# Two transformer blocks: the root of the query/key norm as logarithm and exponential, and a new order of steps around it

## The reference, cut to what matters

```python
def rms_norm(x, g):
    xf = x.astype(jnp.float32)
    y = xf * lax.rsqrt(jnp.mean(xf * xf, axis=-1, keepdims=True) + RMS_EPS)
    return (y * g.astype(jnp.float32)).astype(x.dtype)

def fox_attention(u, w_in, b_f, q_norm_g, k_norm_g, w_out):      # 16 heads of 64, 1024 tokens
    q, k, v, g, fl = jnp.split(u @ w_in, ...)
    q = rms_norm(q, q_norm_g) * (FOX_HD ** -0.5)
    k = rms_norm(k, k_norm_g)
    f_cum = jnp.cumsum(jax.nn.log_sigmoid(fl + b_f), axis=1)
    s = q @ k.T + f_cum[t] - f_cum[s]                            # causal
    o = softmax(s) @ v
    return (o * jax.nn.sigmoid(g)) @ w_out

# in each layer, after the mixer:
x = layer_norm(ALPHA * x + gate * y, ln_g[layer, 0], ln_b[layer, 0])
y = jnp.square(jax.nn.relu(u @ mlp_w1[layer] + mlp_b1[layer])) @ mlp_w2[layer] + mlp_b2[layer]
```

## Time and profile before

| | |
|---|---|
| median of 3 runs | 3938.67 us (3938.32 to 3942.71) |
| the profiled execution, its own time | 3946.69 us |
| its span in the profile | 3945.0 us |
| PE busy | 3705.5 us (94%), 18038 matmuls |
| DVE, ACT, POOL busy | 2020.8 us (51%), 1143.6 us (29%), 2117.1 us (54%) |
| TensorE clock granted, mean | 0.97 |

### The profile page before, as it was taken

How to read it: one execution, slowest core, us unless ns; L and a number is a source line. 1 busy time by engine, 2 the same in 40 slices (tenths; PEclk the granted TensorE clock), 3 DMA queues, 4 the chain that set the end, 5 groups by cost and what they waited for, 6 DMA issues and landing times. The chain is left out here.

```text
span 3945.0 us, 49917 instructions
## 1 busy us (share of the span) xinstructions
PE 3705.5 (94%) x18038; PEld 2988.6 (76%) x18038; DVE 2020.8 (51%) x3309; ACT 1143.6 (29%) x1852; POOL 2117.1 (54%) x1786
## 2 busy tenths in 40 slices
PE   6898989999999889999988999999998889999997
PEld 5677877888888667777766878888787768888886
DVE  6864463333344567777765122222499564444445
ACT  5432231111112544455433111111315132222222
POOL 3643368666663333333326866665495495646462
PEclk8999989999999999999998999999999999999999
DMA  6320112333220011111111211111021111212121
GB/s 223 98 86 27 33 43 70 99 101 97 90 85 23 23 38 38 44 43 39 43 38 32 59 48 48 48 48 48 27 59 43 43 39 52 64 32 64 33 62 43
DMA packets 248500, 224.57 MB, mean 57 GB/s; under 512 B 12660, under 2 KB 194578, under 8 KB 248355
## 3 DMA queue, kind: packets, MB, share of 16 engines
q1 hardware_dynamic: 222240, 171.09, 14.4%
q10 hardware_dynamic: 26115, 51.53, 4.2%
HBM read 218.33 MB, written 4.26 MB: 56 GB/s over the span
## 5 line engine op out<-in xcount | busy, mean ns | idle before, releaser
L3164 POOL TENSOR_SCALAR WH<-RAW 128x1024 fp32r<-128x1024 f32 x255 | 721.1, 2828 | 1034.0 <-issue 342.8
L713 PE MATMUL PS<-UH,WH 128*128 128x512 f32 (+1 forms) x2192 | 866.4, 395 | 21.9 <-POOL WL L3167 14.2
L715 PE MATMUL PS<-UH,WL 128*128 128x512 f32 (+1 forms) x2192 | 860.2, 392 | 0.0
L714 PE MATMUL PS<-UL,WH 128*128 128x512 f32 (+1 forms) x2192 | 859.9, 392 | 0.0
L3167 POOL TENSOR_TENSOR WL<-RAW,WH 128x256 fp32r<-128x256 f32 x1017 | 790.1, 808 | 21.3
L2183 DVE TENSOR_TENSOR X<-PS,X 128x512 f32<-128x512 f32 x432 | 292.5, 687 | 436.2 <-PE PS L845 424.3
L713 PEld LDWEIGHTS PS<-UH,WH 128*128 128x128 f32 (+1 forms) x2192 | 414.7, 189 | 114.6 <-issue 13.9
L715 PEld LDWEIGHTS PS<-UH,WL 128*128 128x128 f32 (+1 forms) x2192 | 414.0, 189 | 89.4
L714 PEld LDWEIGHTS PS<-UL,WH 128*128 128x128 f32 (+1 forms) x2192 | 414.7, 189 | 86.7 <-issue 0.2
L843 PE MATMUL PS<-WH,HH 128*128 128x512 f32 x1024 | 404.4, 395 | 16.8 <-DVE X L2183 13.4
L844 PE MATMUL PS<-WH,HL 128*128 128x512 f32 x1024 | 399.7, 390 | 0.0
(11 more groups left out here) (360 smaller groups left out, 6194.8 us busy)
## 6 DMA issues: line engine op xcount, KB each, us to landing
RAW<-in_mlp_w_dram SPq DMA_DIRECT2D x128, 512.0 KB, 4.0
ADM<-in_ada_w_dram ACTq DMA_DIRECT2D x96, 256.0 KB, 2.9
RAW<-in_w_up_dram SPq DMA_DIRECT2D x44, 512.0 KB, 3.9
ADR<-in_ada_w_dram ACTq DMA_DIRECT2D x32, 512.0 KB, 3.9
WR<-in_od_w_in_dram SPq DMA_DIRECT2D x32, 512.0 KB, 4.3
RAW<-in_w_down_dram SPq DMA_DIRECT2D x22, 512.0 KB, 3.3
RAW<-in_ev_w_in_dram SPq DMA_DIRECT2D x20, 512.0 KB, 3.9
RAW<-in_w_in_dram SPq DMA_DIRECT2D x20, 512.0 KB, 3.9
```

Source lines behind the costliest of these rows:

```text
L713: pe.matmul(bank(b)[0:width], wh, xh, start=(k == 0), stop=False)
L714: pe.matmul(bank(b)[0:width], wh, xl, start=False, stop=False)
L715: mm = pe.matmul(bank(b)[0:width], wl, xh, start=False, stop=(k == NK - 1))
L3164: pool.tensor_scalar(WH[slot][:, 0:n], r[:, 0:n], 1.0, None, ALU.mult).then_inc(S("w_hi"), 1)
```

## The change

Six things, all in the order of work or in the root:

- `root` becomes a logarithm and an exponential with scale -0.5 on ACT, with a semaphore between; the reciprocals of the norm on DVE (`inverse`) go.
- The opening of the odd layer: sums for q stand inside the k column, sums for k ahead of v, the scores of step 0 ahead of g.
- Step 7 of each pair: `values` moves ahead of the `item`, which is cut 3 and 5 instead of 4 and 4; ACT rounds k and DVE makes its low part ahead of `turned`.
- `out_lo` moves from after the division and `normalise` to between the negation and the division.
- The residual rows of pair 0: DVE does two (in steps 1 and 3) instead of four (steps 0 to 3), POOL six instead of four.
- In the MLPs `down` takes each bank just before the first matmul into it, and ACT does `relu` ahead of the modulation DMAs.

```diff
--- before.py
+++ after.py
@@ -194,7 +194,8 @@
...
 NSLOT, NRAW = 9, 2
-RES_DVE = {1: 4, 2: 4, 3: 4, 4: 0, 5: 2}
+RES_DVE = {1: 4, 2: 2, 3: 4, 4: 0, 5: 2}
+RESID_STEPS = (1, 3)
 FL_SLOT = 9
@@ -247,7 +248,7 @@
...
 OD_FIRST = [("k", 0, 0), ("q", 0, 0), ("sk", 0, 0), ("v", 0, 0), ("sq", 0, 0), ("f", 0, 0), ("vt", 0, 0), ("g", 0, 0),
-            ("f", 0, 1), ("q", 0, 1), ("k", 0, 1), ("sq", 0, 1), ("v", 0, 1), ("sk", 0, 1), ("g", 0, 1), ("vt", 0, 1)]
+            ("f", 0, 1), ("q", 0, 1), ("sq", 0, 1), ("k", 0, 1), ("sk", 0, 1), ("v", 0, 1), ("vt", 0, 1), ("g", 0, 1)]
 OD_LAST = [("o", 7, j) for j in (11, 12, 0, 1, 2, 3, 4, 5, 6, 7, 13, 14, 15)]
@@ -827,13 +828,16 @@
...
                 def down(quad, h, first, take=0):
-                    banks = [d_bank() for _ in quad]
+                    banks = []
                     for q in range(2):
...
                             w_ready.take(take)
-                        for b, (tb, mh) in zip(banks, quad):
+                        for j, (tb, mh) in enumerate(quad):
+                            if q == 0:
+                                banks.append(d_bank())
+                            b = banks[j]
                             x = slice((tb % 4) * P, (tb % 4 + 1) * P)
@@ -1218,15 +1222,16 @@
...
                 t_gate(2)
-                item(("k", 0, 1), every)
+                item(("k", 0, 1), lo)
                 head_sums(("sq", 0, 1))
+                item(("k", 0, 1), hi)
+                head_sums(("sk", 0, 1))
                 item(("v", 0, 1), every)
-                head_sums(("sk", 0, 1))
+                scores(0, "hi")
+                turn_v(("vt", 0, 1))
+                scores(0, "lo")
                 item(("g", 0, 1), every)
-                turn_v(("vt", 0, 1))
                 pe.wait_ge(S("t_free"), T_AT["g", 2, 1] + 1)
-                scores(0, "hi")
-                scores(0, "lo")
                 for s in range(64):
@@ -1236,13 +1241,17 @@
...
                         scores(s + 1, "hi")
+                    if s % 8 == 7:
+                        values(s)
+                    cut = 3 if s % 8 == 7 else 4
                     if piece is not None:
-                        item(piece, lo)
+                        item(piece, range(cut))
                     if s < 63:
                         scores(s + 1, "lo")
-                    values(s)
+                    if s % 8 < 7:
+                        values(s)
                     if piece is not None:
-                        item(piece, hi)
+                        item(piece, range(cut, NK))
                     for key in units[1:2]:
@@ -1749,6 +1758,7 @@
...
                         for i in range(4):
+                            relu(it + 1, h, i)
                             for k in (2 * i, 2 * i + 1) if l == 0 else ():
@@ -1757,7 +1767,6 @@
...
                                               [k, :, bass.ds(it * HALF, HALF)]).then_inc(S(f"ada_in{k % 2}"), 16)
-                            relu(it + 1, h, i)
                         if l == 0:
@@ -1813,8 +1822,9 @@
...
                     b = w_take(key)
-                    act.activation(QSQ[(name[1], n, h) in OD_SIDE][:, :], b, ACT.Sqrt, bias=EPSR[:, :], scale=1.0 / 64)\
-                        .then_inc(S("od_wa"), 1)
+                    q = QSQ[(name[1], n, h) in OD_SIDE][:, :]
+                    chain.done(act.activation(q, b, ACT.Ln, bias=EPSR[:, :], scale=1.0 / 64))
+                    act.activation(q, q, ACT.Exp, scale=-0.5).then_inc(S("od_wa"), 1)
@@ -1904,22 +1914,24 @@
...
                 t_gate(2)
+                evict(("sq", 0, 1))
                 evict(("k", 0, 1))
-                evict(("sq", 0, 1))
+                evict(("sk", 0, 1))
                 act.wait_ge(S("negf_out"), 16)
...
                 load_nf(0, 0)
+                round_qk("q", 0, 1)
+                round_qk("k", 0, 1)
                 evict(("v", 0, 1))
-                evict(("sk", 0, 1))
-                round_qk("q", 0, 1)
-                evict(("g", 0, 1))
-                round_qk("k", 0, 1)
                 evict(("vt", 0, 1))
...
                 exp(0, 1)
+                evict(("g", 0, 1))
                 for s in range(64):
...
                     _, first, piece = odd_step(p, i)
+                    if i == 7 and p < 7:
+                        round_qk("k", p + 1, 0)
                     turned(s, 0)
@@ -1929,7 +1941,6 @@
...
                         load_nf(p + 1, 0)
-                        round_qk("k", p + 1, 0)
                     elif i == 1 and p:
@@ -2587,14 +2598,9 @@
...
-                def inverse(name, n, h, part):
+                def normalise(name, n, h):
                     dve.wait_ge(S("od_wa"), OD_FREED["s" + name, n, h][1])
-                    rs = QSQ[(name, n, h) in OD_SIDE][:, part]
-                    chain.done(dve.reciprocal(rs, rs))
-                def normalise(name, n, h):
@@ -2693,11 +2699,8 @@
...
-                whole, parts = slice(0, HALF), (slice(0, 256), slice(256, HALF))
-                inverse("k", 0, 0, whole)
                 normalise("k", 0, 0)
                 ul(2, 1, 0, 1)
-                inverse("q", 0, 0, whole)
                 normalise("q", 0, 0)
@@ -2707,9 +2710,7 @@
...
                 remainder("q", 0, 0)
-                inverse("q", 0, 1, whole)
                 normalise("q", 0, 1)
-                inverse("k", 0, 1, whole)
                 normalise("k", 0, 1)
@@ -2721,6 +2722,8 @@
...
                     units, _, _ = odd_step(p, i)
+                    if i == 7 and p < 7:
+                        remainder("k", n, 0)
                     turned(s, 0)
@@ -2734,27 +2737,28 @@
...
                             scores(s + 1, 1, "hi")
-                    if i in (3, 5, 7) and p < 7:
-                        remainder(*{3: ("q", n, 1), 5: ("k", n, 1), 7: ("k", n, 0)}[i])
+                    if i in (3, 5) and p < 7:
+                        remainder("q" if i == 3 else "k", n, 1)
                     elif i == 1 and p:
                         remainder("q", p, 0)
-                    step = None
-                    if 1 <= i and p < 7:
-                        step = (("q", n, 1), ("k", n, 1), ("k", n, 0), ("q", n, 0))[(i - 1) // 2] + (parts[(i - 1) % 2],)
-                    elif i == 0 and p:
-                        step = ("q", p, 0, parts[1])
+                    ready = {2: ("q", n, 1), 4: ("k", n, 1), 6: ("k", n, 0)}.get(i) if p < 7 else None
+                    if i == 0 and p:
+                        ready = ("q", p, 0)
+                    def between():
+                        if i == 4:
+                            out_lo(p, 1)
+                        elif i == 0 and p:
+                            out_lo(p - 1, 0)
                     if s < 63:
-                        next_scores(s + 1, None if step is None else lambda: inverse(*step))
-                    if step is not None and step[3] is parts[1]:
-                        normalise(*step[0:3])
-                    if i == 4:
-                        out_lo(p, 1)
-                    elif i == 0 and p:
-                        out_lo(p - 1, 0)
+                        next_scores(s + 1, between)
+                    if ready is not None:
+                        normalise(*ready)
                     for key in units[1:2]:
                         out_unit(key)
-                    if p == 0 and i < RES_DVE[2]:
-                        resid(2, i)
+                    if p == 0 and i in RESID_STEPS:
+                        resid(2, RESID_STEPS.index(i))
                 gated(7, 0)
```

## The result

The changed kernel takes 3900.66 us (median of four runs, 3899.64 to 3904.03); the kernel before, on the same chip, 3938.56 us (3938.32 to 3942.71). The ratio is 0.9903, with a 95% interval of 0.9886 to 0.992: 37.9 us, or 1.0%, faster. Forecast were 44.0 us and 3894.7 us. The profiled execution of the changed kernel took 3900.26 us, its span is 3898.5 us.

A forecast was written before the change was run, and what follows sets the result against it. PE, busy 94% of the span, was taken as the bound, so only its idle time could be won. Terms 15.4 + 2.2 + 1.3 + 0.7 + 5.3 + 19.1 = 44.0 us; median 3938.7 - 44.0 = 3894.7 us, range 3880 to 3922.

The forecast's parts named there:

- part 1: `down` in both MLPs: PE's waits for banks go, 15.4 us won in the second MLP and 2.2 in the first.
- part 2: First MLP, `relu` ahead of DMA issues: one PE wait for HL goes, 1.3 us; later DMAs cost 0.
- part 3: Odd layer's root: DVE loses 14 us of reciprocals a pair; ACT keeps two table loads per root, none at the softmax.
- (c): Rival, odd layer's roots: logarithm and exponential share one table, so the load between them goes; 3893.4 us, chance 0.06.
- (d): Rival, odd layer: a third table load stays in front of the softmax exponential; 3899.6 us, chance 0.03.
- parts 4 and 5: Odd layer's opening, 0.7 us won (bounds -3 and +4), and pair 0, 5.3 us won from shorter waits and the clock.
- The stall of 3.1 us: Opening: behind the first root, ACT frees PE's transposition banks later because of table loads; PE loses 3.1 us.
- 2.8 + 1.0: Opening, new order: the transposition comes 2.8 us earlier, plus 1 us of slow matmuls after the long wait saved.
- part 6: Steady pairs and last pair: shorter PE waits for the division, KL and MOL, 19.1 us won in sum.
- 6.9 + 2.2 us: Steady pairs, `out_lo` ahead of the division: six MOL waits shortened by 1.15 us each, six smaller ones 2.2 in all.
- (a): Rival: odd-layer waits are shifted, not removed; half of pair 0's and later pairs' gain goes, 12 us: 3907, chance 0.22.
- (b): Rival: 192 new waits inside `down` break the matmul stream; at 0.30 us each 3952 us; chance 0.06 full, 0.12 partial.

The follow-up runs named there:

- the `down` kernel: The kernel before with one edit, `down` asking for each bank just before the first matmul into it: 3928.44 us, ratio 0.9964.

## Why the prediction was right, and where it was not

**`down` (part 1, 17.6 us).** The mechanism was right and so was 0 for the new waits. Measured 13.4 and 2.8 us. The term of the second MLP was 2.0 us too large; what failed is that "the first has long been added, and each later one has 1.4 us more" looks at banks only. PE, being earlier, met the weight tiles twice, 3.2 us; the forecast asked what is late next in the steady pairs, but not here.

**`relu` (part 2, 1.3 us).** Measured 2.9. I priced the one wait of the earlier trace rows. With lazily taken banks PE comes earlier to `up`'s output and waits for HL six times, so the part is worth more beside part 1 than the trace of before could show; the 2 us at which the later DMAs were bounded don't appear.

**The root (part 3).** Two loads per root and none at the softmax: 64 were expected, 64 are there, so (c) and (d) didn't come true in this kernel. The Trainium skill, page "ScalarE: Activation LUTs", section "Table sets: the hidden batching unit", has one set with both functions, so that a logarithm followed by an exponential needs one load. The trace disagrees: here a load stands between the two each time (31 and 32 rows of 1.28 us above).

**Opening and pair 0 (parts 4 and 5, 6.0 us together).** Measured 4.2. The stall of 3.1 us is there with 3.05 and costs 3.6 to 3.9 in all by the traces; the matmuls after it run slower (last section). Of the new order I expected 2.8 + 1.0; undoing it costs 3.1 by the traces. The waits around the first scores went as laid out: of 6.5 us 3.9 are left (2.0 for the squares, 0.9 for KL, 1.0 for MXT). As separate numbers, 0.7 won in the opening and 5.3 in pair 0, they were wrong (4.6 lost and 8.8 won). The term that failed is the clock. I gave 1.0 us of slow matmuls back to the opening and a part of 2.3 us to pair 0. Measured, PE's busy time grew by 4.4 us in the opening and fell by 5.8 us in pair 0, and the two nearly cancel. That the sum came out near is luck to this extent.

**Steady pairs and last pair (part 6, 19.1 us).** Measured 15.2, and here the sum was better than its reasons. The waits went as forecast, the weight tile is what was late next (0.67 us a pair where 0.4 were left over by the forecast's account), and no wait of L740 without releaser is left in the steady pairs. But I gave 6.9 + 2.2 us to `out_lo` ahead of the division and 3.5 to KL ahead of the additions. The kernel with the root alone has none of these waits either: each of them was VectorE being late by its reciprocals, 14 us a pair. The order alone ends those for MOL and KL as well, but gets another one for it, for PT. The move of `out_lo` is worth 3 us in six pairs beside the new root. The reason by which the earlier trace rows was read, what stands in front of the subtraction, was right; that the reciprocal is one of the things in front of it, and goes, was used for the division and not for MOL. In the last pair 2.6 us were expected and 1.1 came, as a new wait of 2.78 us for PT took the place of the old ones.

**Rivals.** (a), waits shifted and not removed, is true on a small scale: 3.2 us in the second MLP, 4.0 in the steady pairs (2.2 of them forecast), 2.8 in the last one. (b) is refuted by the `down` kernel. The four misses (-3.9 in the pairs, -2.0 in the second MLP, -1.8 around pair 0, +2.1 in the first MLP) add to the 5.6 us by which the changed stretches fall short of 44.0.

## What to carry to other kernels

When several waits of the bottleneck engine go back to one engine that is late, they are one cause: price each cure with the others in place, for the first takes nearly all (89.66 against 89.45 us a pair here) and a reordering alone can be worth nothing (91.91 against 91.80). An instruction that fits the free time of an engine by its sum may still not fit at its place: 3.35 us of reciprocal in one piece cost 57 us over the kernel that had none, in halves 21. And an activation function is chosen place by place: logarithm and exponential paid in the pairs, where VectorE was late, and cost 3.6 us or more by the traces in the opening, where the square root's table was already in place.

## What the runs showed of the hardware

**VectorE beside GpSimd.** In the changed kernel the same normalisation of 128x512, with both operands in SBUF, takes 0.74 us in the 16 cases with no GpSimd instruction beside it, 1.23 on the mean of the 13 that mostly overlap GpSimd's subtractions of L3171, and 2.85 in the one that started 0.44 us after the product of L3165. It ended 0.55 us after that product (1979.72 and 1979.17), as if it had waited for its end. It did so in five more traces (2.82 to 2.85 us, each started 0.44 or 0.45 us after the product). The 13 behave alike: each ended 0.55 us after the subtraction that had begun before it, which took 0.73 to 0.86 us. The Trainium skill, page "SBUF — State Buffer", section "SBUF: two separate sides", has a VectorE instruction with two SBUF inputs and a GpSimd instruction that reads SBUF exclude each other, and the one that starts first keeps the other out for its whole length; by that rule, the 2.85 and the 1.23 us agree.

The traces disagree with it beside GpSimd's rounding to the high part, an instruction with one input from SBUF: the last pair's normalisation took 0.74 to 0.75 us in the five traces in which it began 0.96 to 1.64 us after such a rounding of 2.77 to 2.97 us (one of them is shown above, at 1969.79 us). So what held the normalisation up in these runs is GpSimd's instructions with two inputs. Why the other kind lets it pass no run shows, and it isn't free for all: VectorE's subtraction for KL, begun 0.28 to 0.43 us after such a rounding, took 1.16 to 1.30 us in four steady pairs, where the median of all 12 in six pairs is 0.69, and still ended more than 1 us ahead of the rounding.

**The clock after a wait.** Behind the wait of 3.05 us the matmuls of the changed kernel start 0.43 us apart, at the lower of the two levels, up to 1279.4 us, and 0.23 apart again soon after it. The granted clock of 1275 to 1280 us is 0.66 and that of 1275 to 1290 us 0.89; in the kernel before both were 1.00. Against 0.23 us each, the starts up to there lose 1.6 us; with the 2.7 us by which the wait is longer than before that would be 4.3 us, of which 3.6 to 3.9 are left at the end of pair 0.

```profile
1277.66 0.63 PE L1111 MATMUL PS<-UH,WH 128*128 128x512 f32 x1
1278.09 0.63 PE L1112 MATMUL PS<-UL,WH 128*128 128x512 f32 x1
...
1279.68 0.40 PE L1113 MATMUL PS<-UH,WL 128*128 128x512 f32 x1
1279.91 0.40 PE L1111 MATMUL PS<-UH,WH 128*128 128x512 f32 x1
```

A second such stretch, 1300.0 to 1306.8 us at a granted clock of 0.50, follows a wait of 1.9 us for UL. The kernel before has the same wait and ran at 1.00 all the way from 1268 to 1343 us, so this wait alone isn't what lowers the clock; what does stays open.

**One execution and another.** Code that is the same took 558.0 to 563.8 us up to the first `down`, and 1117.6 to 1121.0 us after the second MLP. A gain of 5 us can't be read from one span. A stretch that holds the change is better, but not all are equally steady: pairs 1 to 6 took 536.7 and 536.8 us in the two profiles of the changed kernel, the second MLP 1.6 us more in one than in the other, and opening with pair 0 differed by 2.7 us where none of its code did.
